# A two-layer diffusion backbone on one NeuronCore: residual stream in two halves, SiLU as one ScalarE function, and constant TensorE products in the stops

## The chip, the cores and the metric

The kernel runs on one core of a Trainium2 chip. The metric is the device time of one execution in microseconds (us); lower is better. Engines are called PE (TensorE), ACT (ScalarE), DVE (VectorE), POOL (GpSimd) and SP (SyncE, which issues most transfers).

## The reference

Two layers over 256 latent and 256 context tokens of width 1024, in float32. Each layer has a mixer (three attention or convolution branches) and a channel mixer, each between two RMS norms, with modulation computed from `c`:

```python
hx = modulate(rmsnorm(x, g_pre_mix[l]), sh1, sc1)
y_x, y_c = mixer_sublayer(hx, hc, ...)
x = x + gt1 * rmsnorm(y_x, g_post_mix[l])
hx = modulate(rmsnorm(x, g_pre_ffn[l]), sh2, sc2)
x = x + gt2 * rmsnorm(channel_mixer(hx, l, ...), g_post_ffn[l])

def swiglu(h, w_gu, w_dn):                  # layer 0, width 2816
    g, u = jnp.split(h @ w_gu, 2, axis=-1)
    return (jax.nn.silu(g) * u) @ w_dn
# layer 1: each token to 2 of 8 experts of width 3584, latent tokens only
```

## The kernel before

Activations lie with channels on partitions: a tensor of width 1024 is 8 tiles (`k`, `KT = 8`) of 128 channels by 512 tokens (latent tokens first, then context). Every product of weights is made in three passes of float32r: ACT copies a weight block to a high part, DVE subtracts it from the raw block to get the low part, and PE multiplies high by high, high by low and low by high. So each 1 MB weight slab goes DMA, ACT (`split_hi` L549, or `hi` L783 for experts), DVE (`split_lo` L835, or `lo` L1230), PE. Five instruction queues are written by hand and joined by semaphores; within a queue the order is that of the code.

The stages, in time: eight slabs of the modulation product `ada` (PE L1307) to 50 us; mixer of layer 0 to 654 us; dense FFN in two halves of 12 and 10 tiles to 1109 us; mixer of layer 1 to 1461 us; router to 1508 us; then a loop over jobs of one expert and 128 token slots (8 jobs in this run, 42 slabs each, 127 us a job) to 2527 us; last norm and output.

Between stages stand norms. `postnorm` (DVE L930 reciprocal, L938, L943) updates the residual `xm` tile by tile; ACT squares each tile (`square`, L584), PE sums it over channels with a product against the constant `mean` (`norm_sum`, L1300, into bank O1; its squares lie in two buffers, so a square waits for the sum two tiles back), ACT takes the root (L578, after a table load), DVE the reciprocal (L896), and `prenorm` scales (DVE L906), shifts (ACT L611) and splits (DVE L917) tile by tile. `first_pair` on PE takes each tile `k` of the split input as soon as it is there, six products a tile. In these stretches PE has nothing to do but wait.

The router (layer 1): 16 transposes of the normed latent tokens (L1546), 16 products with 8 columns for the logits (L1551), a chain of small DVE operations, five products with 8 columns (L1556 to L1560), more small DVE operations, one more product (L1563) and the reading of the job count, then `gather` (16 products, L1571), which builds the tokens of the first job.

SiLU is made as x(1+tanh(x/2))/2: ACT tanh from PSUM (L730 dense, L805 experts), then on DVE two `scalar_tensor_tensor` (L1085 and L1086, or L1253 and L1255). In an expert job the 28 gate/up slabs go in 14 groups `q` of two slabs; in each, DVE does two `lo`, the two SiLU operations, and one split of the transposed result (L1246). The 14 down slabs follow; in the first of them DVE also prepares the one-hot matrices of the next job (L1210 to L1218). Three split buffers (`wse`) stand between ACT/DVE and PE.

The residual `xm` is `[P, KT, TOK]`; its context half is free in the expert stage and serves as the sixth raw slab buffer, eight pieces of 1 KB a partition. The output is written from the latent half, also eight pieces of 1 KB.

Of the kernel before, what the change touches and what calls it, by code (L numbers as in the profile page):

```python
# [28 lines left out]
P = 128  # L29
# [114 lines left out]
def build_program(nc, a, out):  # L144
    ctx = ExitStack()
    with ctx:
# [11 lines left out]
        xm = sb("xm", [P, KT, TOK])  # L158
# [31 lines left out]
        def ada_rows(n):  # L190
# [21 lines left out]
                 view(M, 8192, 8, 256), view(M, 10240, 8, 256), view(M, 12288, 8, 256), xm[:, :, SEQ:TOK]]  # L212
# [50 lines left out]
        tanh_done, gu_taken, hF_done = sem("tanh_done"), sem("gu_taken"), sem("hF_done")  # L263
# [6 lines left out]
        e_tanh, e_h, e_T, e_hThi, e_hT = sem("e_tanh"), sem("e_h"), sem("e_T"), sem("e_hThi"), sem("e_hT")  # L270
# [156 lines left out]
        def _(sp):  # L427
# [74 lines left out]
            sp.dma_start(out, xm[:, :, 0:SEQ]).then_inc(out_done, 16)  # L502
# [37 lines left out]
        def _(act):  # L540
# [39 lines left out]
            def square(src, n, k, N):  # L580

                if 8 * n + k >= 2:
                    act.wait_ge(sum_done, 8 * n + k - 1)
                act.activation(sq[:, k % 2, 0:N], src, ACT.Square).then_inc(sq_done, 1)  # L584

            def ada():
                split_to(1)
                for s in range(ADA_FIRST):
# [3 lines left out]
                    for k in FIRST_NORM[s]:  # L592
                        if k == 0:
                            act.wait_ge(x_in, 16)
                        square(xm[:, k, :], 0, k, TOK)

            def prenorm(n, l, which, N, hcount):
                if n == 0:
                    act.wait_ge(eps_ready, 3)
                else:  # L600
                    for k in range(KT):
                        act.wait_ge(x_upd, 8 * hcount[0] + k + 1)
                        square(xm[:, k, 0:N], n, k, N)
# [115 lines left out]
            def ffn():  # L719
                for h in range(2):  # L720
# [74 lines left out]
            with act.Fori(0, n_jobs) as j:  # L795
# [5 lines left out]
                for q in range(GU_GROUPS):  # L801
# [3 lines left out]
                    act.activation(tge[:, q % 2, :], S[q % 2][:, 0:256], ACT.Tanh, scale=0.5).then_inc(e_tanh, 1)  # L805
# [23 lines left out]
        def _(dve):  # L829
# [64 lines left out]
            def prenorm(n, l, which, N):  # L894
# [3 lines left out]
                for k in range(KT + 1):  # L898
                    if k < KT:
# [4 lines left out]
                        for s in range(ns):  # L904
                            c = slice(SEQ * s, SEQ * s + SEQ)
                            ins = dve.scalar_tensor_tensor(gt[:, k % 2, c], xm[:, k, c], am[:, 2 * which, k, s:s + 1],  # L906
# [20 lines left out]
            def postnorm(n, l, which, N, src):  # L927
# [6 lines left out]
                for k in range(KT + 1):  # L934
# [4 lines left out]
                    if k:  # L939
                        dve.wait_ge(dve_self, at[k - 1])  # L940
                        for s in range(N // SEQ):
                            c = slice(SEQ * s, SEQ * s + SEQ)
                            ins = dve.scalar_tensor_tensor(xm[:, k - 1, c], gt3[:, (k - 1) % 3, c], am[:, 2 * which + 1, k - 1, s:s + 1],  # L943
                                                           xm[:, k - 1, c], ALU.mult, ALU.add)
# [57 lines left out]
            def mixer(l):  # L1002
                nq = TOK if l == 0 else SEQ

                mg = xm if l == 0 else xm[:, :, SEQ:TOK]
# [64 lines left out]
            def ffn():  # L1070
                for h in range(2):
# [6 lines left out]
                    def body(i, last):  # L1078
                        for s in range(2):
# [3 lines left out]
                            dve.wait_ge(tanh_done, f0 + 2 * i + s + 1)  # L1083
# [10 lines left out]
                    body.own_per = 4  # L1094
# [146 lines left out]
            with dve.Fori(0, n_jobs) as j:  # L1241
                own.base, own.jobs_done = start + j * (GU_GROUPS + 10), j + 1
# [22 lines left out]
                assert own.k == GU_GROUPS + 10  # L1265
# [5 lines left out]
            own.base, own.k = start + n_jobs * (GU_GROUPS + 10), 0  # L1271
# [6 lines left out]
        def _(pe):  # L1278
# [528 lines left out]
```

## Time and profile before

| | |
|---|---|
| median of three runs | 2555.19 us (2554.53 to 2555.3) |
| the profiled execution's own time | 2547.89 us |
| its span, first to last instruction | 2545.8 us |
| busy PE / DVE / ACT | 2375.2 / 1746.2 / 1341.0 us |
| mean granted TensorE clock | 0.974 of full |

Busy shares are over the whole span; PE's matmuls are pipelined and their ends are modelled, so a busy PE row can still hide slack of some tenths of a microsecond. The granted clock is 1.00 (2.4 GHz) or 0.50 (1.2 GHz) in any short stretch.

### The profile page before, as it was taken

What the parts mean: (1) busy time and instruction counts of PE and PEld (TensorE: products, weight loads), DVE (VectorE), ACT (ScalarE), POOL (GpSimd) and SP (SyncE); (2) the same over time, 40 slices, a digit from 0 to 9 for tenths busy, and PEclk for the clock granted to TensorE, in tenths of its full rate; (3) what the DMA queues carried; (4) which work ended last, traced back from release to release, by engine and by line L of the source; (5) the groups of instructions that cost most, each with busy time, mean ns of one, the idle gap of its engine ahead of it and who ended that gap; (6) DMA issues with size and microseconds to landing.
All of it is one profiled execution on the core that took longest, in us unless ns stands there. A gap on an engine that the chain in (4) does not pass through costs nothing.

```text
span 2545.8 us, 34852 instructions
## 1 busy us (share of the span) xinstructions
PE 2375.2 (93%) x12536; PEld 1941.4 (76%) x12536; DVE 1746.2 (69%) x2249; ACT 1341.0 (53%) x1636; POOL 28.6 (1%) x26
## 2 busy tenths in 40 slices
PE   5988999999799999978999869999999999999997
PEld 3766877777488788757899858888888888888885
DVE  5565456543655345466656469898989898989897
ACT  5334445432444233234445347676767676767674
POOL 0000000000000000000011000000000000000000
PEclk9989999999899999989999979999999999999999
DMA  6222333333144244313244449898989898989894
GB/s 226 70 97 100 117 108 108 116 116 116 54 161 165 99 144 153 111 55 116 100 130 136 170 152 368 326 369 325 369 326 369 325 369 325 368 326 367 326 367 164
DMA packets 128776, 528.62 MB, mean 208 GB/s; under 512 B 9136, under 2 KB 68016, under 8 KB 75440
## 3 DMA queue, kind: packets, MB, share of 16 engines
q1 hardware_dynamic: 126096, 520.86, 55.9%
q10 hardware_dynamic: 2592, 6.55, 0.8%
q8 instruction: 59, 0.97, 0.1%
q14 instruction: 29, 0.24, 0.0%
HBM read 526.33 MB, written 1.05 MB: 207 GB/s over the span
## 4 chain that ended last, share of the span: by engine, by line
PE 84%; DVE 9%; ACT 4%; issue 2%; DMA 1%; ACTq 0%; DVEq 0%; SPq 0%
PE O L1626 11%; PE pp L1283 9%; PE pp L1284 8%; PE pp L1285 8%; PE S L1604 8%; PE S L1602 8%; PE S L1603 8%; PE pp L1307 3%; PE O L1300 2%; DVE wsp L835 2%; PE S L1283 2%; PE T L1283 1%; PE S L1284 1%; PE T L1284 1%; PE S L1285 1%
## 5 line engine op out<-in xcount | busy, mean ns | idle before, releaser
L835 DVE TENSOR_TENSOR wsp<-raw,wsp 128x1024 fp32r<-128x1024 f32 (+3 forms) x344 | 378.6, 1125 | 477.8 <-ACT wsp L549 473.3
L1230 DVE TENSOR_TENSOR opr<-M,opr 128x2048 fp32r<-128x2048 f32 x168 | 383.5, 2287 | 30.0 <-ACT opr L783 27.1
L549 ACT ACTIVATE wsp<-raw 128x1024 fp32r<-128x1024 f32 (+3 forms) x344 | 322.2, 966 | 122.3 <-PE T L1285 81.2
L783 ACT ACTIVATE opr<-M 128x2048 fp32r<-128x2048 f32 x168 | 322.6, 1920 | 91.9 <-PE O L1626 52.0
L1602 PE MATMUL S<-opr,hx 128*128 128x512 f32 x896 | 359.0, 401 | 2.3 <-DVE hx L1235 2.2
L1604 PE MATMUL S<-opr,hx 128*128 128x512 f32 x896 | 350.3, 391 | 0.0
L1603 PE MATMUL S<-opr,hx 128*128 128x512 f32 x896 | 349.4, 390 | 0.0
L1283 PE MATMUL pp<-hx,wsp 128*128 128x512 f32 (+1 forms) x800 | 286.7, 358 | 41.4 <-DVE wsp L835 15.7
L1626 PE MATMUL O<-opr,wsp 128*128 128x512 f32 x1344 | 311.5, 391 | 12.9 <-DVE opr L1230 12.9
L1626 PEld LDWEIGHTS O<-opr,wsp 128*128 128x128 f32 x1344 | 250.5, 188 | 67.7 <-DVE opr L1230 16.3
L1284 PE MATMUL pp<-hx,wsp 128*128 128x512 f32 (+1 forms) x800 | 279.9, 350 | 0.0
L1285 PE MATMUL pp<-hx,wsp 128*128 128x512 f32 (+1 forms) x800 | 279.4, 349 | 0.0
L1230 DVE TENSOR_TENSOR opr<-raw,opr 128x2048 fp32r<-128x2048 f32 x114 | 261.0, 2290 | 19.5 <-ACT opr L783 14.6
L783 ACT ACTIVATE opr<-raw 128x2048 fp32r<-128x2048 f32 x114 | 219.0, 1921 | 49.2 <-PE O L1626 25.6
L1283 PEld LDWEIGHTS pp<-hx,wsp 128*128 128x128 f32 x800 | 155.5, 194 | 66.9 <-issue 33.3
L1283 PE MATMUL pp<-opr,wsp 128*128 128x512 f32 (+1 forms) x496 | 185.7, 374 | 12.9 <-DVE opr L1065 9.9
L1604 PEld LDWEIGHTS S<-opr,hx 128*128 128x128 f32 x896 | 168.2, 188 | 35.8
L1602 PEld LDWEIGHTS S<-opr,hx 128*128 128x128 f32 x896 | 168.3, 188 | 34.8 <-issue 2.4
L1603 PEld LDWEIGHTS S<-opr,hx 128*128 128x128 f32 x896 | 168.7, 188 | 32.4
L1284 PE MATMUL pp<-opr,wsp 128*128 128x512 f32 (+1 forms) x496 | 177.9, 359 | 0.0
L1285 PE MATMUL pp<-opr,wsp 128*128 128x512 f32 (+1 forms) x496 | 177.7, 358 | 0.0
L1285 PEld LDWEIGHTS pp<-hx,wsp 128*128 128x128 f32 x800 | 155.1, 194 | 19.5
(203 smaller groups left out, 3374.1 us busy)
## 6 DMA issues: line engine op xcount, KB each, us to landing
M<-in_w_moe SPq DMA_DIRECT2D x168, 1024.0 KB, 4.9
raw<-in_w_main SPq DMA_DIRECT2D x132, 1024.0 KB, 4.9
raw<-in_w_moe SPq DMA_DIRECT2D x114, 1024.0 KB, 4.9
xm<-in_w_moe SPq DMA_DIRECT2D x56, 1024.0 KB, 5.7
raw<-in_w_br SPq DMA_DIRECT2D x24, 512.0 KB, 3.6
raw<-in_w_dn SPq DMA_DIRECT2D x8, 768.0 KB, 4.1
raw<-in_w_dn SPq DMA_DIRECT2D x8, 640.0 KB, 3.8
M<-in_rpb_rows ACTq DMA_DIRECT2D x16, 256.0 KB, 2.9
```

Source lines behind the costliest of these rows:

```text
L549: act.activation(wsp[:, slot, 0, 0:w], raw[:, slot // 2, half * w:half * w + w], ACT.Copy).then_inc(hi_done, 1)
L783: act.activation(wse[i % SPLIT_E][:, 0, :, :], raw_e[i % RAW_E], ACT.Copy).then_inc(e_hi, 1)
L835: dve.tensor_tensor(wsp[:, slot, 1, 0:w], raw[:, slot // 2, half * w:half * w + w], wsp[:, slot, 0, 0:w], ALU.subtract).then_inc(lo_done, 1)
L1230: dve.tensor_tensor(w[:, 1, :, :], raw_e[i % RAW_E], w[:, 0, :, :], ALU.subtract).then_inc(e_lo, 1)
L1283: mm(dst, w_hi, x_hi, start=first, stop=False)
L1284: mm(dst, w_hi, x_lo, start=False, stop=False)
L1285: return mm(dst, w_lo, x_hi, start=False, stop=last)
L1307: ins = mm(dst[0:4, 0:256], c4[:, 4 * h + k, :], wsp[:, slots[h], part, 256 * k:256 * k + 256], start=(h + k + part == 0), stop=(h == 1 an ...
L1602: mm(d, xg[0][:, kk, :], wh, start=(kk == 0), stop=False)
L1603: mm(d, xg[0][:, kk, :], wl, start=False, stop=False)
L1604: ins = mm(d, xg[1][:, kk, :], wh, start=False, stop=(kk == KT - 1))
L1626: ins = mm(O[n][:, :].rearrange("p (a b) -> p a b", b=256), hT[x][:, f, :], w[:, part, 4 * f2 + 2 * n:4 * f2 + 2 * n + 2, :], start=(f == ...
```

## The change

1. `xm` becomes `[P, 2, KT, SEQ]`: latent half, then context half, so that each half is 8 KB contiguous in a partition. The host array `x_both` and all readers and writers follow; the sixth expert slab and the output become one row of 8 KB.
2. SiLU: ACT evaluates `Silu` instead of `Tanh`, and DVE has one `tensor_tensor` with the up product instead of two `scalar_tensor_tensor`.
3. `keep_up(n)` puts `n` products of the constant `mean` with itself (128x128, float32) into PSUM bank T1, which nothing reads, at eleven places in PE's queue ahead of a wait.

```diff
-        xm = sb("xm", [P, KT, TOK])
+        xm = sb("xm", [P, 2, KT, SEQ])
...
-                 view(M, 8192, 8, 256), view(M, 10240, 8, 256), view(M, 12288, 8, 256), xm[:, :, SEQ:TOK]]
+                 view(M, 8192, 8, 256), view(M, 10240, 8, 256), view(M, 12288, 8, 256), xm[:, 1, :, :]]
...
-            sp.dma_start(out, xm[:, :, 0:SEQ]).then_inc(out_done, 16)
+            sp.dma_start(out, xm[:, 0, :, :]).then_inc(out_done, 16)
...
-                            act.activation(gt[:, s, :], S[s][:, :], ACT.Tanh, scale=0.5).then_inc(tanh_done, 1)
+                            act.activation(gt[:, s, :], S[s][:, :], ACT.Silu).then_inc(silu_done, 1)
...
-                            own.link(dve.scalar_tensor_tensor(gt[:, s, :], gt[:, s, :], 1.0, S[s][:, :], ALU.add, ALU.mult))
-                            dve.scalar_tensor_tensor(hf2[:, s, :], gt[:, s, :], 0.5, T[s][:, :], ALU.mult, ALU.mult
-                                                     ).then_inc(gu_taken, 1)
+                            dve.tensor_tensor(hf2[:, s, :], gt[:, s, :], T[s][:, :], ALU.mult).then_inc(gu_taken, 1)
...
-                    dve.wait_ge(e_tanh, j * GU_GROUPS + (q + 1))
-                    own.link(dve.scalar_tensor_tensor(tge[:, q % 2, :], tge[:, q % 2, :], 1.0, S[q % 2][:, 0:256],
-                                                      ALU.add, ALU.mult))
-                    dve.scalar_tensor_tensor(hse[:, q % 2, :], tge[:, q % 2, :], 0.5, S[q % 2][:, 256:512],
-                                             ALU.mult, ALU.mult).then_inc(e_h, 1)
+                    dve.wait_ge(e_silu, j * GU_GROUPS + (q + 1))
+                    dve.tensor_tensor(hse[:, q % 2, :], tge[:, q % 2, :], S[q % 2][:, 256:512], ALU.mult).then_inc(e_h, 1)
...
+            def keep_up(n):
+
+                for _ in range(n):
+                    mm(T[1][:, 0:P], mean[:], mean[:], start=True, stop=True)
...
             ada()
+            keep_up(32)
             mixer(0, 1, 0)
+            keep_up(34)
             for k in range(KT):
                 norm_sum(2, k, TOK)
+            keep_up(31)
             ffn()
+            keep_up(32)
             for k in range(KT):
                 norm_sum(4, k, TOK)
+            keep_up(31)
             mixer(1, 5, 2)
+            keep_up(21)
             for k in range(KT):
                 norm_sum(6, k, SEQ)
+            keep_up(31)
...
+            keep_up(11)
             pe.wait_ge(rt_dve, 2)
...
+            keep_up(20)
...
-            gather(0)
+            gather(0, 14)
+            keep_up(8)
```

PE's queue at the router, before (L1300 is `norm_sum`; L1546 the transposes; L1551 the logits; L1556 to L1563 the small products; L1564 reads the job count; L1571 is `gather`):

```order
L1300 MATMUL O<-M,mean 128x256 x10
L1546 MATMUL pp<-ident,M 128x128 x8
L1546 MATMUL S<-ident,M 128x128 x8
L1551 MATMUL O<-wr,M 128x8 x16
L1556 MATMUL O<-M,ctab 128x8
L1557 MATMUL O<-M,ctab 128x8
L1558 MATMUL O<-M,ctab 128x8
L1559 MATMUL O<-M,ctab 128x8
L1560 MATMUL O<-M,ctab 128x8
L1563 MATMUL O<-M,ctab 128x8
L1564 TENSOR_LOAD jobs
```

The same place in the changed kernel, where L1299 is `keep_up`, L1303 `norm_sum`, L1556 the transposes, L1561 the logits, L1567 to L1575 the small products and L1584 `gather`:

```order
L1303 MATMUL O<-M,mean 128x256 x8
L1299 MATMUL T<-mean 128x128 x31
L1556 MATMUL pp<-ident,M 128x128 x8
L1556 MATMUL S<-ident,M 128x128 x8
L1561 MATMUL O<-wr,M 128x8 x16
L1299 MATMUL T<-mean 128x128 x11
L1567 MATMUL O<-M,ctab 128x8
L1568 MATMUL O<-M,ctab 128x8
L1569 MATMUL O<-M,ctab 128x8
L1570 MATMUL O<-M,ctab 128x8
L1571 MATMUL O<-M,ctab 128x8
L1299 MATMUL T<-mean 128x128 x20
```

Nothing is moved there; runs of constant products stand between the old rows, each ahead of a row that waits for DVE or ACT. Behind them, 14 more stand ahead of `gather` and 8 behind it.

ACT's queue at the head of the expert loop, before (L783 is `hi`, L805 the tanh, the other rows registers):

```order
L795 UNCONDITIONAL_BRANCH
L795 ISA
L782 ISA
L783 ACTIVATE opr<-M 128x2048
L782 REGISTER_ALU
L783 ACTIVATE opr<-M 128x2048
L804 REGISTER_ALU
L805 ACTIVATE M<-S 128x256
L783 ACTIVATE opr<-M 128x2048
```

The same place in the changed kernel, where L786 is `hi` and L808 the SiLU:

```order
L798 UNCONDITIONAL_BRANCH
L798 ISA
L785 ISA
L786 ACT_TABLE_LOAD
L786 ACTIVATE opr<-M 128x2048
L785 REGISTER_ALU
L786 ACTIVATE opr<-M 128x2048
L807 REGISTER_ALU
L808 ACT_TABLE_LOAD
L808 ACTIVATE M<-S 128x256
L786 ACTIVATE opr<-M 128x2048
```

Two loads of activation tables have come into the loop's body, ahead of its first `hi` and ahead of its first SiLU; they stand there once a job. In the first dense half's loop (five passes) one load stood ahead of the first `split_hi`; in the changed kernel a second stands ahead of the first SiLU of each pass:

```order
L549 ACT_TABLE_LOAD
L549 ACTIVATE wsp<-raw 128x1024
L548 REGISTER_ALU
L549 ACTIVATE wsp<-raw 128x1024
L732 REGISTER_ALU
L733 ACT_TABLE_LOAD
L733 ACTIVATE M<-S 128x512
```

## Rows read from the trace of the kernel before

**Rows 1.** Stretches: us, busy PE, PEld, DVE, ACT, POOL, clock, DMA share, GB/s.

```profile
658.00:668.00 10.00, 6.11 (x7) 2.38 (x8) 9.96 (x20) 3.04 (x5) 0.00 (x0) 0.50 0.00 0
1477.00:1483.00 6.00, 3.44 (x16) 3.45 (x17) 1.77 (x4) 3.97 (x8) 0.00 (x0) 0.50 0.41 130
1484.00:1487.00 3.00, 3.00 (x28) 2.94 (x27) 0.00 (x0) 1.17 (x1) 0.00 (x0) 1.00 1.00 423
1488.00:1504.00 16.00, 5.73 (x25) 5.57 (x26) 11.15 (x50) 2.12 (x2) 1.80 (x1) 0.50 0.03 14
```

**Rows 2.** Chain that ended last, by time, in the first mixer's `first_pair`.

```profile
64.43 0.88 DVE M L906 x2
...
66.20 0.88 DVE M L906 x2
```

**Rows 3.** Timeline at the FFN start: start, us, engine, line [idle before, releaser].

```profile
670.61 0.63 ACT L584 ACTIVATE M<-xm 128x512 f32<-128x512 f32 x1 [0.41 <-PE O L1300]
690.19 1.28 ACT L549 ACT_TABLE_LOAD   x1
691.49 2.01 ACT L549 ACTIVATE wsp<-raw 128x1024 fp32r<-128x1024 f32 x2
693.88 1.99 ACT L549 ACTIVATE wsp<-raw 128x1024 fp32r<-128x1024 f32 x2
695.00 2.01 PE L1307 MATMUL pp<-wsp,c 128*4 128x256 f32 x16 [1.76 <-DVE wsp L835]
```

**Rows 4.** Timeline of PE, and a row of DVE, last mixer to first expert.

```profile
1466.11 6.39 PE L1300 MATMUL O<-M,mean 128*128 128x256 f32 x16 [4.79 <-ACT M L584]
1469.51 0.88 DVE L943 SCALAR_TENSOR_TENSOR xm<-M,am,xm 128x256 f32<-128x256 f32 x2
1479.56 1.97 PE L1546 MATMUL pp<-ident,M 128*128 128x128 f32 x8 [7.06 <-ACT M L611]
1483.03 4.00 PE L1551 MATMUL O<-wr,M 128*128 128x8 f32 x32
1489.85 0.59 PE L1556 MATMUL O<-M,ctab 128*128 128x8 f32 x2 [2.83 <-DVE M L1164]
1490.30 0.57 PE L1557 MATMUL O<-M,ctab 128*128 128x8 f32 x2
1497.02 0.56 PE L1563 MATMUL O<-M,ctab 128*128 128x8 f32 x2 [4.86 <-DVE M L1202]
1501.13 5.32 PE L1571 MATMUL pp<-M 128*128 128x128 f32 x32 [3.55 <-DVE M L1218]
1508.67 0.49 PE L1602 MATMUL S<-opr,hx 128*128 128x512 f32 x1 [2.22 <-DVE hx L1235]
```

**Rows 5.** Timeline at the end of the first dense half.

```profile
844.00 0.69 DVE L1086 SCALAR_TENSOR_TENSOR M<-M,T 128x512 f32<-128x512 f32 x1
846.23 0.49 PE L1283 MATMUL pp<-opr,wsp 128*128 128x512 f32 x1 [1.20 <-DVE opr L1092]
```

**Rows 6.** Timeline at the head of an expert job.

```profile
1629.29 3.73 PE L1571 MATMUL pp<-M 128*128 128x128 f32 x32
1634.03 1.91 ACT L783 ACTIVATE opr<-M 128x2048 fp32r<-128x2048 f32 x1
1639.24 1.92 ACT L783 ACTIVATE opr<-M 128x2048 fp32r<-128x2048 f32 x1 [3.30 <-PE S L1604]
1641.96 0.38 ACT L805 ACTIVATE M<-S 128x256 f32<-128x256 f32 x1 [0.80 <-PE S L1604]
1644.19 2.29 DVE L1230 TENSOR_TENSOR opr<-M,opr 128x2048 fp32r<-128x2048 f32 x1
```

**Rows 7.** Waits from 1515 to 2525 us: total, times, longest.

```profile
PE O L1626 <- DVE opr L1230: 12.9, 8, 1.6
```

**Rows 8.** DMA issues: KB each, us from issue to landing.

```profile
M<-in_w_moe SPq DMA_DIRECT2D x168, 1024.0 KB, 4.9
...
xm<-in_w_moe SPq DMA_DIRECT2D x56, 1024.0 KB, 5.7
```

More of the change, by code:

```diff
@@ L262, in build_program @@
         bias_in, bias_ready = [sem("bias_in0"), sem("bias_in1")], sem("bias_ready")
-        tanh_done, gu_taken, hF_done = sem("tanh_done"), sem("gu_taken"), sem("hF_done")
+        silu_done, gu_taken, hF_done = sem("silu_done"), sem("gu_taken"), sem("hF_done")
         act_self, dve_self, pool_self = sem("act_self"), sem("dve_self"), sem("pool_self")
@@ L583, in square @@
                     act.wait_ge(sum_done, 8 * n + k - 1)
-                act.activation(sq[:, k % 2, 0:N], src, ACT.Square).then_inc(sq_done, 1)
+                dst = sq[:, k % 2, 0:N]
+                if len(src.shape) == 3:
+                    dst = dst.rearrange("p (a b) -> p a b", b=SEQ)
+                act.activation(dst, src, ACT.Square).then_inc(sq_done, 1)
             def ada():
@@ L594, in ada @@
                             act.wait_ge(x_in, 16)
-                        square(xm[:, k, :], 0, k, TOK)
+                        square(xm[:, :, k, :], 0, k, TOK)
             def prenorm(n, l, which, N, hcount):
@@ L602, in prenorm @@
                         act.wait_ge(x_upd, 8 * hcount[0] + k + 1)
-                        square(xm[:, k, 0:N], n, k, N)
+                        square(xm[:, :, k, :] if N == TOK else xm[:, 0, k, :], n, k, N)
                 norm_root(n, N)
@@ L804, in _ @@
                     act.wait_ge(e_used, j * JOB_SLABS + (2 * q + 2 + SPLIT_E))
-                    act.activation(tge[:, q % 2, :], S[q % 2][:, 0:256], ACT.Tanh, scale=0.5).then_inc(e_tanh, 1)
+                    act.activation(tge[:, q % 2, :], S[q % 2][:, 0:256], ACT.Silu).then_inc(e_silu, 1)
                     if q == 1:
@@ L905, in prenorm @@
                             c = slice(SEQ * s, SEQ * s + SEQ)
-                            ins = dve.scalar_tensor_tensor(gt[:, k % 2, c], xm[:, k, c], am[:, 2 * which, k, s:s + 1],
+                            ins = dve.scalar_tensor_tensor(gt[:, k % 2, c], xm[:, s, k, :], am[:, 2 * which, k, s:s + 1],
                                                            rs[:, c], ALU.mult, ALU.mult)
@@ L942, in postnorm @@
                             c = slice(SEQ * s, SEQ * s + SEQ)
-                            ins = dve.scalar_tensor_tensor(xm[:, k - 1, c], gt3[:, (k - 1) % 3, c], am[:, 2 * which + 1, k - 1, s:s + 1],
-                                                           xm[:, k - 1, c], ALU.mult, ALU.add)
+                            ins = dve.scalar_tensor_tensor(xm[:, s, k - 1, :], gt3[:, (k - 1) % 3, c], am[:, 2 * which + 1, k - 1, s:s + 1],
+                                                           xm[:, s, k - 1, :], ALU.mult, ALU.add)
                             if s == N // SEQ - 1:
@@ L1003, in mixer @@
                 nq = TOK if l == 0 else SEQ
-                mg = xm if l == 0 else xm[:, :, SEQ:TOK]
+                mg = xm[:].rearrange("p s (h k) c -> p (s h) (k c)", k=2) if l == 0 else xm[:, 1, :, :]
                 for row in mixer_steps[l]:
@@ L1093, in body @@
                             dve.wait_ge(hF_done, f0 + 2 * i + s + 1)
-                    body.own_per = 4
+                    body.own_per = 2
                     loop(dve, n, body, own)
@@ L1241, in _ @@
             with dve.Fori(0, n_jobs) as j:
-                own.base, own.jobs_done = start + j * (GU_GROUPS + 10), j + 1
+                own.base, own.jobs_done = start + 10 * j, j + 1
                 def hT_lo(q):
@@ L1264, in _ @@
                 xg_lo(j + 1)
-                assert own.k == GU_GROUPS + 10
+                assert own.k == 10
                 for n in range(4):
@@ L1270, in _ @@
                                       ALU.add).then_inc(e_acc, 1)
-            own.base, own.k = start + n_jobs * (GU_GROUPS + 10), 0
+            own.base, own.k = start + n_jobs * 10, 0
             postnorm(7, 1, 1, SEQ, yacc)
@@ L1564, in _, with gather @@
             n_jobs = pe.value_load(jobs[0:1, 12:13], min_val=1, max_val=MAX_JOBS)
-            def gather(j):
+            def gather(j, idle=0):
+                keep_up(idle)
                 pe.wait_ge(e_onehot, j + 1)
@@ L1782, in _lay_out @@
         "w_main": w_main, "w_br": w_br, "w_dn0": w_dn0, "w_dn1": w_dn1, "w_moe": _pack_experts(inp),
-        "x_both": tok.T.reshape(KT, P, TOK).transpose(1, 0, 2),
+        "x_both": tok.T.reshape(KT, P, 2, SEQ).transpose(1, 2, 0, 3),
         "c_both": np.stack([inp["c"][0], inp["c_ctx"]], axis=1).reshape(KT, P, 2).transpose(1, 0, 2),
```

4 lines of the change are left out of this document (2 added, 2 removed).

## The prediction

> **What bounds the kernel now.** I read the page first: PE is busy for 93% of the span and its mean granted clock is 0.974, so what is left is short waits and a little half-rate work. Then the table of stretches, to find where the clock is low: the long stops between stages and the whole router are at 0.50 [rows 1]. Then the chain that ended last, by time, to see whether the half-rate products are on the path, and the timelines for what follows a stop.
>
> Between stages it is mostly not PE's clock that counts. In the first mixer's `first_pair` the chain goes through DVE, one tile every 1.77 us (64.43 to 66.20) [rows 2]; PE needs for a tile six products of 0.23 us at full clock, 1.4 us, or 2.6 us at half. It starts behind by what the half clock costs and has caught up before the last tile. In the router it is otherwise: PE, DVE and ACT take turns, each waits for the one before, and every half-rate product lies on the path [rows 4]. In the expert stage PE runs nearly without gap; its one wait is 12.9 us in 8 jobs, for a low part that DVE makes late because it builds the one-hot matrices first [rows 7].
>
> **The constant products.** First, do they fit? One is a 128x128 float32 product like those of `gather`: 16 take 3.73 us with the last one's tail at full clock, so 0.223 us each [rows 6]. The eleven runs then take 7.1, 7.6, 6.9, 7.1, 6.9, 4.7, 6.9, 2.5, 4.5, 3.1 and 1.8 us. The stops in the router are 4.79, 7.06, 2.83, 4.86, 3.55 and 2.22 us [rows 4], and of the 3.55 PE spends part on reading the job count; I charge 0.1 us there. The stops between stages of 512 tokens are of the length of the 7.06 one or longer. Nothing else stands in the way: T1 is not read then. Each run starts at full clock, as the clock falls only some microseconds into a stop.
>
> Do they hold the clock? In 658 to 668 us products of the same stationary `mean` ran at 0.50 and the clock came back behind them [rows 1]; `gather`, of the very form of a constant product, started at 0.50 at 1501 and had the clock back at 1504 [rows 1, 4]. I take yes.
>
> What it gives, place by place:
> - The three `first_pair`: nothing where DVE sets the end [rows 2]. The pair of layer 1's mixer, where PE is behind nearly to the last tile, 0.1 us.
> - `norm_sum` at 662 us: the last square waited 0.41 us for PE [rows 3]; I take 0.2. At 1116 us the last square waits for DVE alone: 0. At 1466 us (256 tokens): the last update of `xm` ends at 1470.39, and one square of 0.42 and one sum of 0.45 behind it would end at 1471.3, plus handovers 1471.6, where the sums now end at 1472.5 [rows 4]: 0.9.
> - Transposes and logits: 1479.56 to 1483.03 at half clock [rows 1, 4], 3.47 us for 16 transposes, so 1.7 saved; the half-rate start of the logits adds 0.3. Together 2.0.
> - The five small products go at 0.45 us start to start (1489.85, 1490.30) at half clock; the logits, of the same form, took 4.00 us for 16 at full, 0.24 each [rows 4]. Saved 0.9.
> - `gather`: 5.32 against 3.73 us at full clock [rows 4, 6]: 1.6. ACT and DVE are free behind it, so the first expert product moves with it.
> Sum 5.7, less the 0.1: 5.6 us.
>
> **SiLU.** DVE loses one operation a tile. In the dense loop and in the expert groups PE is the bound, so that is hidden, except at two ends. At the end of a dense half PE waits for the last tile's split, 1.20 us in the first half, with the 0.69 us operation in the chain [rows 5]: 0.7 saved, and 0.65 in the second, whose stop I take as about as long. At the start of the down stage of a job the low part that PE waits for comes after a `hi` of ACT which itself waits for PE, so DVE's new slack is cut to 0.06 us a job: 0.5 in eight.
>
> ACT pays with table loads of 1.28 us [rows 3]: one more in each of five passes of the dense loop, two in each of eight jobs. In a dense pass the second load falls into ACT's wait for the gate tile, 24 products of PE, and is hidden. Not so in the first pass: ACT's highs of 693.88 go to about 695.3 behind load and SiLU, the first low part behind them is ready at 697.6, and PE is done with its modulation product at 697.0 (695.00 + 2.01) [rows 3]. Cost 0.6, once. At a job's head the first load delays the `hi` of 1634.03 to end at 1637.3, when DVE has just become free. The second starts when the `hi` of 1639.24 ends, at 1641.16, and ends at 1642.44 instead of the SiLU's 1641.96: 0.48 us late. The next `hi` (1.92) and `lo` (2.29) then end at 1647.0; PE wants that slab at 1641.96 - 0.2 + 2 x 2.72 + 0.4 = 1647.6 (a slab takes 2.72, the distance of the two ACT waits) [rows 6]. Hidden, with half a microsecond to spare. In the first job, where nothing is prepared ahead, I charge 0.3.
>
> The Trainium skill's "ScalarE: Activation LUTs", section "What ACT_TABLE_LOAD costs", adds a drain of about 1.38 us to each switch, 2.66 us in all, and says to group functions by set. In the row the `split_hi` starts 0.02 us behind the load's end [rows 3], so I let the trace decide; by the rule each job would lose 0.9 us and the sum would shrink by 7.
>
> SiLU itself I take to last as long as tanh (0.38 us) [rows 6]; no row shows it. If it lasted twice that, the head's slack would be just used up: 0 to 1 us.
>
> **Layout.** A slab written in 1 KB pieces lands in 5.7 us, one in 8 KB pieces in 4.9 [rows 8]. In the expert stage nobody waits for it, so 0. The output transfer is last on the path and of the same size: between 0 and 0.8 saved, I take 0.6, near the rows. ACT and DVE read the same number of elements: 0.
>
> **Sum.** 5.6 + 1.35 + 0.5 - 0.6 - 0.3 + 0.6 = 7.15 us. The profiled execution took 2547.89 us, 2545.8 of it span; 2540.7 after. The runs shown have a median 7.3 us above that execution, so 2548.0 us.
>
> **Rivals.**
> - *The clock falls inside the router.* [...] If it lasts one run: 11 x 0.446 - 2.83 = 2.1 over, and 0.9 not gained: 2551. If it stays low to `gather`: 2.1 + (8.9 - 4.86) + (6.2 - 3.55) + (3.6 - 2.22) = 10.2 over and 2.5 not gained, which ends at 2548.0 + 12.7 = 2560.7, slower. It decides against the change once the clock stays low through the second run. [...] Against: 31 constant products stand ahead and the clock came back at `gather`.
> - *The constant products don't hold the clock at all*, the change does not do what it says. Then all eleven overrun, 4 to 8 us in each of seven long stops: above 2590. Against: rows 1.
> - *The table loads reach the path.* Half a microsecond of slack at each head; with a load of 2.66 instead of 1.28, 0.9 x 8 = 7 us lost: 2555, no change.
> - *PE was held by its clock more than the chain shows*, so that each of the five half-rate stretches gives another microsecond: 2543.
>
> The Trainium skill's "TensorE: Matmul & The Clock Gate", section "Part 4: PE-mode transpose", says that a transpose does not count as busy to the clock gate; with the transposes and logits in a row that would speak for the first rival, and give its 2551. In the trace the clock rose behind the transposes at 1483 [rows 1], which speaks against it.
>
> **Numbers.** Forecast 0.53; one fall in the router 0.13; low to `gather` 0.08; no hold 0.04; loads on the path 0.12; more gain 0.10. The range goes from 2543.5 to 2555. About 0.2% (5.1 us) can be told from no change here: faster below 2550.1. The forecast falls there in nine cases of ten, the extra gain always, the single fall in one of three: 0.63. Slower: low to `gather` and no hold: 0.12. Same: 0.25.
>
> **What would show it.** After: clock 1.00 from 1461 us to the end of the router and the router some 5.5 us shorter; `first_pair` as long as before; 33 table loads; jobs still 127 us apart; an idle PE of under 1 us at each dense half's end. Wrong if the clock is 0.50 in any run of constant products, if jobs come at 128 us, or if the spacing of tiles in `first_pair` changes.

## The result, and the profile after

| | before | after |
|---|---|---|
| median, first comparison (4 runs each) | 2555.24 us (2554.53 to 2555.3) | 2540.46 us (2539.94 to 2541.04) |
| profiled execution | 2547.89 us | 2541.04 us |
| its span | 2545.8 us | 2538.6 us |
| mean granted clock | 0.974 | 0.989 |
| busy PE / DVE / ACT | 2375.2 / 1746.2 / 1341.0 us | 2424.3 / 1693.7 / 1368.0 us |

The ratio is 0.9943, 95% interval 0.9926 to 0.996: 14.8 us less, where 7.2 were forecast, and 2540.46 lies below the range of 2543.5 to 2555. Yet the two profiled executions differ by 6.85 us, close to the forecast sum of 7.15. The step from the one to the other is taken up below; a part of the 14.8 us stays unexplained.

The table of stretches of after, at the places of [rows 1] and the stretch ahead of the router (columns as there):

```profile
658.00:668.00 10.00, 8.66 (x34) 4.00 (x32) 10.00 (x23) 3.78 (x6) 0.00 (x0) 1.00 0.00 0
1461.00:1477.00 16.00, 15.71 (x110) 12.82 (x110) 12.55 (x26) 7.37 (x17) 0.00 (x0) 1.00 0.07 17
1477.00:1483.00 6.00, 5.87 (x54) 5.68 (x53) 0.42 (x2) 4.25 (x7) 0.00 (x0) 1.00 0.63 240
1484.00:1487.00 3.00, 2.73 (x26) 2.54 (x24) 2.38 (x15) 0.20 (x1) 0.00 (x0) 1.00 1.01 418
1488.00:1504.00 16.00, 14.78 (x121) 14.09 (x121) 10.78 (x39) 5.47 (x5) 1.81 (x1) 1.00 0.18 67
```

The clock is 1.00 where it was 0.50. The timeline of PE through the router, to be laid beside [rows 4] (L1299 is `keep_up`):

```profile
1470.80 7.08 PE L1299 MATMUL T<-mean 128*128 128x128 f32 x62
1478.02 1.09 PE L1556 MATMUL pp<-ident,M 128*128 128x128 f32 x8
...
1479.82 3.64 PE L1561 MATMUL O<-wr,M 128*128 128x8 f32 x32
1483.31 2.70 PE L1299 MATMUL T<-mean 128*128 128x128 f32 x22
1486.28 0.39 PE L1567 MATMUL O<-M,ctab 128*128 128x8 f32 x2 [0.27 <-DVE M L1165]
```

Eight transposes take 1.09 us, not 1.97. The runs fit their stops: 0.27 us is left ahead of the small products. From the first transpose to the first small product it is 8.3 us (10.3 before), from there to the first expert product 16.3 (18.8 before). From the first square (1464.87) to the first expert product (1502.57) the router now takes 37.7 us, and 43.0 before.

In the first mixer's `first_pair` DVE's tiles come as they did in [rows 2], 1.78 us apart (timeline of DVE):

```profile
64.19 0.88 DVE L909 SCALAR_TENSOR_TENSOR M<-xm,am,M 128x256 f32<-128x256 f32 x2
65.96 0.88 DVE L909 SCALAR_TENSOR_TENSOR M<-xm,am,M 128x256 f32<-128x256 f32 x2
```

The dense stage's start, timeline of ACT and one row of PE, beside [rows 3]:

```profile
688.47 1.28 ACT L549 ACT_TABLE_LOAD   x1
689.76 2.01 ACT L549 ACTIVATE wsp<-raw 128x1024 fp32r<-128x1024 f32 x2
691.78 1.28 ACT L733 ACT_TABLE_LOAD   x1
693.08 0.60 ACT L733 ACTIVATE M<-S 128x512 f32<-128x512 f32 x1
...
693.27 2.01 PE L1310 MATMUL pp<-wsp,c 128*4 128x256 f32 x16 [1.90 <-DVE wsp L838]
```

Two loads stand where one stood, and each is followed 0.01 or 0.02 us behind its end by the next ACTIVATE. The trace of after has 35 loads (14 before; 33 were forecast). The first product of the down stage of the first half waits 0.46 us where it waited 1.20 [rows 5]:

```profile
844.68 0.49 PE L1281 MATMUL pp<-opr,wsp 128*128 128x512 f32 x1 [0.46 <-DVE opr L1093]
```

The head of an expert job (timeline of ACT), beside [rows 6], then the waits of PE in the expert stage beside [rows 7], then the transfers beside [rows 8], and the output transfer:

```profile
1628.40 1.28 ACT L786 ACT_TABLE_LOAD   x1
...
1633.48 1.92 ACT L786 ACTIVATE opr<-M 128x2048 fp32r<-128x2048 f32 x1 [1.88 <-PE S L1618]
1635.42 1.28 ACT L808 ACT_TABLE_LOAD   x1
1636.71 0.38 ACT L808 ACTIVATE M<-S 128x256 f32<-128x256 f32 x1
```

```profile
PE O L1640 <- DVE opr L1231: 12.6, 8, 1.6
```

```profile
M<-in_w_moe SPq DMA_DIRECT2D x168, 1024.0 KB, 4.9
...
xm<-in_w_moe SPq DMA_DIRECT2D x56, 1024.0 KB, 5.0
...
out_x<-xm SPq DMA_DIRECT2D x1, 1024.0 KB, 3.9
```

SiLU lasts as long as the tanh, 0.38 us. The slab in `xm` lands in 5.0 us (5.7 before), the output in 3.9. The first operation of DVE's preparation of a next job, in the first and in the eighth job, before and then after (timeline of DVE):

```profile
1594.07 0.28 DVE L1210 TENSOR_SCALAR M<-ctab,M 128x128 f32<-128x128 f32 x1
...
2483.17 0.28 DVE L1210 TENSOR_SCALAR M<-ctab,M 128x128 f32<-128x128 f32 x1
```

```profile
1588.32 0.28 DVE L1211 TENSOR_SCALAR M<-ctab,M 128x128 f32<-128x128 f32 x1
...
2477.02 0.28 DVE L1211 TENSOR_SCALAR M<-ctab,M 128x128 f32<-128x128 f32 x1
```

Seven jobs take 889.10 us before and 888.70 after: 0.06 us less each, as forecast.

Two stretches changed in a way that was not forecast. The first mixer (from its first weights to the first square behind it) takes 603.9 us before and 600.8 after, the second (from the first square ahead of it to the first behind it) 350.0 and 351.6. The traces of e1, e4 and e9 below have the same signs: 603.6 and 349.7 in e1, the kernel before, 601.8 and 354.4 in e4, 602.1 and 354.4 in e9, the changed kernel. No run here isolates the cause.

### The profile page after: what moved, and what is told of

Its sections match the earlier page's. It is cut to its first block, busy times and chain, and to the rows that moved or that the text cites. A ratio compares the mean times of both kernels' runs of the same rounds, so it can differ in the third digit from the quotient of the medians.

```text
span 2538.6 us, 35669 instructions
## 1 busy us (share of the span) xinstructions
PE 2424.3 (95%) x13066; PEld 1987.4 (78%) x13066; DVE 1693.7 (67%) x2115; ACT 1368.0 (54%) x1657; POOL 27.0 (1%) x26
## 4 chain that ended last, share of the span: by engine, by line
PE 81%; DVE 11%; ACT 4%; issue 3%; DMA 0%; ACTq 0%; DVEq 0%; SPq 0%
PE O L1640 11%; PE pp L1281 8%; PE S L1618 8%; PE S L1616 8%; PE S L1617 8%; PE pp L1283 8%; PE pp L1282 8%; PE pp L1310 3%; DVE wsp L838 2%; PE S L1281 2%; PE S L1283 2%; PE T L1283 2%; PE T L1281 1%; PE S L1282 1%; PE T L1282 1%
## 5 line engine op out<-in xcount | busy, mean ns | idle before, releaser
L786 ACT ACTIVATE opr<-M 128x2048 fp32r<-128x2048 f32 x168 | 322.5, 1920 | 81.0 <-PE O L1640 51.5
L1283 PE MATMUL pp<-hx,wsp 128*128 128x512 f32 (+1 forms) x800 | 277.0, 346 | 0.0
L786 ACT ACTIVATE opr<-raw 128x2048 fp32r<-128x2048 f32 x114 | 219.1, 1922 | 48.2 <-PE O L1640 25.6
L1281 PE MATMUL pp<-opr,wsp 128*128 128x512 f32 (+1 forms) x496 | 186.0, 375 | 10.7 <-DVE opr L1068 9.3
L1283 PE MATMUL pp<-opr,wsp 128*128 128x512 f32 (+1 forms) x496 | 178.1, 359 | 0.0
L1283 PEld LDWEIGHTS pp<-hx,wsp 128*128 128x128 f32 x800 | 153.6, 192 | 18.9
```

The costliest lines, as they stand in the source:

```text
L786: act.activation(wse[i % SPLIT_E][:, 0, :, :], raw_e[i % RAW_E], ACT.Copy).then_inc(e_hi, 1)
L1281: mm(dst, w_hi, x_hi, start=first, stop=False)
L1283: return mm(dst, w_lo, x_hi, start=False, stop=last)
```

## The experiments

Each session timed its kernels on one chip beside the kernel before, which thus has four more sets of runs: medians 2552.86 (26 runs), 2554.24 (22), 2555.98 (11) and 2554.16 (11).

### First session: the parts alone

e1 is the kernel before with no edit. e2 has only part 3 of the change (the `keep_up` calls), e3 only parts 1 and 2 (layout and SiLU), e4 all of it:

```diff
 # e3, and so at all eleven places
-            keep_up(32)
             mixer(0, 1, 0)
-            keep_up(34)
...
 # e2, the same calls put into the kernel before
+            keep_up(32)
             mixer(0, 1, 0)
+            keep_up(34)
```

> The kernel before, unchanged. The forecast's sum (7.15 us) fits the two profiled executions (2547.89 to 2541.04), yet the timed runs of before lie at 2555. Theory A: before has executions of two kinds that differ only in where the clock falls; then some of these runs lie near 2548 and some near 2555, with spans 7 us apart and a lower mean clock in the longer ones. Theory B (rival): the profiled execution of before was a stray; all runs here lie at 2555 and the profile too. Then the forecast's step from span to median was right, and the change is worth 14 us by something the sum doesn't hold.

> Constant products alone, at all eleven places; tanh and the old layout stay. My sum: 5.6 us off a like execution of before. If theory A holds (clock falls vary from run to run), the gain over the median is 5.6 + 7 = 12 to 13 us, since these products take away most of the falls: about 2542 to 2543, and all runs agree within 1 us. If the additional gain is not the clock's, 2549.5.

> Layout and SiLU as in the changed kernel, no constant products. My sum: 1.55 us off before. Theory A: 2553.7 in the runs of the longer kind (2546 in a short one), with as many clock falls as before. Rival: if SiLU or the layout is what the sum lacks, 2546 in all runs.

> All three parts, the changed kernel again on the same chip as the others: 2540.5, runs within 1 us.

| | median (runs) | ratio to before | profiled: span, clock |
|---|---|---|---|
| e1, before | 2554.72 (11) | 1.0006 [0.9997, 1.0015] | 2550.3, 0.972 |
| e2, constant products | 2544.89 (9) | 0.9968 [0.9958, 0.9978] | 2542.3, 0.989 |
| e3, layout and SiLU | 2553.78 (11) | 1.0 [0.9991, 1.0009] | 2553.5, 0.970 |
| e4, all | 2543.63 (6) | 0.9969 [0.9957, 0.9981] | 2540.3, 0.989 |

e1 came out as neither theory says: its executions and the 26 beside them make no two groups 7 us apart but lie spread over 11 us, at granted clocks of 0.970 to 0.974. e2 missed: 8.0 us less and not 12 to 13, and its nine runs lie 7.4 us apart and not 1. e3's median is as expected. e4 missed: 3.1 us above the expected time, its runs 4.4 us apart and not 1.

The constant products hold nearly the whole gain. Here it is 9.2 us by medians, not 14.8, and the 26 executions of before lie between 2548.04 and 2558.88 us: the profiled execution of before, 2547.89, was shorter than all of them (three of the later sessions were shorter still). e1's profile shows one place where executions of this kernel differ. Stretches of e1 in the router, beside the lower three of [rows 1] (same columns):

```profile
1477.00:1483.00 6.00, 2.13 (x10) 2.14 (x11) 2.67 (x7) 4.08 (x10) 0.00 (x0) 0.64 0.12 31
1484.00:1487.00 3.00, 3.00 (x17) 3.00 (x15) 0.00 (x0) 2.21 (x3) 0.00 (x0) 0.50 1.03 434
1488.00:1504.00 16.00, 6.04 (x27) 5.79 (x27) 8.51 (x48) 2.12 (x2) 1.80 (x1) 0.50 0.13 53
```

And the timeline of PE there:

```profile
1482.63 1.91 PE L1546 MATMUL S<-ident,M 128*128 128x128 f32 x8
1484.34 6.83 PE L1551 MATMUL O<-wr,M 128*128 128x8 f32 x32
```

In [rows 1] the clock was back at 1.00 in 1484 to 1487 us and the logits took 4.00 us; in e1 it stays at 0.50 and they take 6.83. e1's router takes 46.3 us, 3.3 more than in the profiled execution of before, and the first mixer's first weights are loaded at 59.34 instead of 57.32 us. That is 5.3 us, of which the span shows 4.5; the rest comes back in the mixers. e3's router is like e1's, 46.9 us with the clock at 0.50 through it. e6's, which has no constant products in the router either, is like that of the profiled before: 43.1.

### Second session: where the constant products work, and the table loads

e5 has the old layout and SiLU with the five router runs only, e6 with the six runs between stages only; e7 is the whole change with an early SiLU of one element; e8 is the new layout and SiLU with the four runs behind the logits only.

```diff
 # e5: only these; e6: only the other six; e8: only the last four of these
+            keep_up(31)                     # ahead of the transposes
+            keep_up(11)                     # behind the logits
+            keep_up(20)
+            gather(0, 14)
+            keep_up(8)
```

```diff
 # e7
+        dum = sb("dum", [P, 2])
...
                 norm_root(n, N)
+                if n == 2:
+                    act.activation(dum[:, 0:1], eps[:], ACT.Silu)
...
             act.activation(rt[:, 8:10], rt[:, 10:12], ACT.Exp).then_inc(rt_act, 1)
+            act.activation(dum[:, 1:2], eps[:], ACT.Silu)
```

> The old layout and the old SiLU, constant products only behind the last norm sum and in the router (31, 11, 20, 14, 8). Theory (the gain lies in the router, and is larger than forecast since a usual execution has the clock low there from 1479 to 1509 us, while the profiled one had it back at 1484): 6.5 to 8.5 us less than the kernel before in the same session, router stretches of 13.1, 8.3 and 16.3 us from the last square to the first expert product, as with all eleven runs. Rival (half of the gain comes from the stops between stages): 3 to 5 us less. Rival (as forecast): 5.4 us less.

> The old layout and the old SiLU, constant products only at the six places between stages (32, 34, 31, 32, 31, 21), none in the router behind the norm sums. Theory (DVE sets the end of these stretches, only the norm sums gain): 0.5 to 1.5 us less than the kernel before in the same session; the router as without the change, its clock low for some 30 us. Rival (PE was held by its clock more than the chain shows, about a microsecond in each of five stretches): 4 to 6 us less.

> The whole change, and a SiLU of one element a partition behind the root of the FFN's norm and behind the router's Exp, so that the SiLU table is loaded where ACT waits for DVE, and no load is left in the dense loop or the job loop (33 loads become 12). Theory (a load costs only where it stands on the chain: at the dense stage's start, 0.9 for the second one and up to 1.3 for the first, and 0.5 in the first job): 1.4 to 2.7 us less than the whole change alone, so 10.6 to 12 us less than the kernel before where the whole change alone gives 9.2; jobs as far apart as before. Rival (loads in the job loop cost 0.3 us or more a job): jobs closer by 0.3 us or more and 4 us less than the whole change. Rival (the loads are all hidden): no difference to the whole change.

> The new layout and SiLU, constant products only from behind the logits on (11, 20, 14, 8), none ahead of the transposes or between the stages. Theory A (the transposes and logits run at half clock, and the following products are dense enough that the clock comes back within the first two runs): the 11 products take up to 4.9 us in a stop of 2.8, small products start up to 2.1 us late, and from the third run on nothing is late: 0 to 3 us more than with the 31 products ahead. Theory B (8-column and short products never bring it back once low): all four runs overrun and the first expert product comes 10 us later than in the whole change.

- **e5**: 2546.73 us, 7.5 less than before; ratio 0.9972 [0.9963, 0.9981]. The router alone gives most of the gain, more than the 5.3 by which the two profiled executions differ there. Its small products came 10.7 us behind the transposes and not the expected 8.3, since the clock fell within the logits and the eleven constant products behind them ran at half rate (5.04 us).
- **e6**: 2551.64 us, ratio 0.9995 [0.9985, 1.0005]. The runs between stages give no difference that can be told, which fits the 0.5 to 1.5 us expected; the rival's 4 to 6 us lie outside the interval. They do hold the clock, and DVE's tiles come 1.78 us apart still (stretches, then the timeline of DVE, of e6):

```profile
60.00:70.00 10.00, 9.41 (x37) 6.21 (x36) 9.21 (x21) 5.21 (x12) 0.00 (x0) 1.00 0.00 1
655.00:665.00 10.00, 9.58 (x71) 7.79 (x69) 8.83 (x13) 2.92 (x5) 0.00 (x0) 1.00 0.00 0
```

```profile
62.29 0.88 DVE L906 SCALAR_TENSOR_TENSOR M<-xm,am,M 128x256 f32<-128x256 f32 x2
64.07 0.88 DVE L906 SCALAR_TENSOR_TENSOR M<-xm,am,M 128x256 f32<-128x256 f32 x2
```

- **e7**: 2542.38 us, 11.9 less than before; ratio 0.9958 [0.9945, 0.9971]. The table is loaded while ACT waits, and the dense loop starts without a load (timeline of ACT, then of PE):

```profile
671.62 1.28 ACT L610 ACT_TABLE_LOAD   x1
...
688.54 1.99 ACT L550 ACTIVATE wsp<-raw 128x1024 fp32r<-128x1024 f32 x2
690.92 0.60 ACT L736 ACTIVATE M<-S 128x512 f32<-128x512 f32 x1 [0.39 <-PE S L1287]
```

```profile
692.03 2.02 PE L1313 MATMUL pp<-wsp,c 128*4 128x256 f32 x16 [0.47 <-DVE wsp L842]
```

  PE's wait ahead of the modulation product falls from 1.90 to 0.47 us. From the first square to the first product of the down stage it is 2.05 us less than in after, the first job is 0.5 shorter, and jobs are as far apart as in after (seven in 888.72 us): behind the first job, the loads in the job loop cost nothing. The trace has 11 loads.
- **e8**: one run, 2544.92 us, span 2543.0. Transposes at half clock (1.97 and 1.91 us), small products 11.5 us behind the start of the transposes, the first expert product 27.7 us behind it, 3.1 more than in after. Its second run of constant products fits its stop again (4.71 us). Theory A, at its upper end. The clock rose within the logits, at about 1483.5 us, as in the profiled before, fell within the eleven constant products (4.33 us) and was back at their end; what was lost ahead of them stays lost.

### Third session: the whole change again, and the stops it leaves out

e9 is the changed kernel, e10 is e7's kernel, e12 has the new layout and SiLU and only the 31 products ahead of the transposes. e11 is e7's kernel with three runs more:

```diff
                 for s in range(ADA_FIRST):
+                    keep_up(14 if s == 2 else 0)
...
                             if i == 0:
+                                keep_up((20, 15)[l])
                                 pe.wait_ge(m_split, 8 * (l + 1))
```

> The whole change once more, beside the kernel before on the same chip. Theory (the first comparison, 14.8 us, met executions of before at the long end of their spread and of after at the short end; the change itself is worth about 9): 8 to 11 us less than the kernel before, median 2542 to 2545. Rival (the change is worth 14.8 and the second session was the odd one): 13 to 16 us less.

> The whole change with the SiLU table loaded ahead of both loops, once more, on the same chip as the whole change alone. Theory (the loads cost 2.0 at the dense stage's start and 0.5 in the first job): 2 to 3 us less than the whole change alone. Rival (what the two profiles differ in is chance): within 1 us.

> The kernel with the loads ahead of the loops, and constant products at three stops more: 14 ahead of the third slab of the modulation product (a stop of 3.9 us near 17 us), 20 and 15 ahead of each mixer's last stage (5.0 and 4.3 us, near 600 and 1430 us). Theory (every fall of the clock in a stop is followed by half-rate work that PE does not make up): no fall at 17, 597 and 1430 us, the end of the first stage at 56.6 instead of up to 58.9 us, 2 to 4 us less than without them, and a smaller spread. Rival (DVE and ACT set the pace there too): the falls vanish and the time stays.

> The new layout and SiLU, and of the constant products only the 31 ahead of the transposes. Theory A (they keep the clock through the transposes and, mostly, the logits, and it falls in the stop behind): transposes at 1.04 us for eight, not 1.97; the small products and the gather at half, so that the first expert product comes 2.5 to 3.5 us later than in the whole change. Theory B (the transposes and logits bring it down at once, as a rule on transposes says): logits at half, 2 us more.

- **e9**: 2544.50 us (6 runs), 11.5 less than before; ratio 0.9956 [0.9944, 0.9968]. Median as expected, the difference half a microsecond above. Its router takes 38.8 us against 37.7 in after: the clock fell within the eleven constant products, at about 1486.9 us, and was back at about 1490.3, within the small ones. These start 0.8 us later behind the transposes than in after, without a wait, and lose another 0.3 (timeline of PE):

```profile
1482.19 3.64 PE L1560 MATMUL O<-wr,M 128*128 128x8 f32 x32
1485.68 3.97 PE L1298 MATMUL T<-mean 128*128 128x128 f32 x22
1489.44 0.43 PE L1566 MATMUL O<-M,ctab 128*128 128x8 f32 x2
```

  In e7, e10, e13 and e15 the clock fell for as long, and the router takes 38.8 us too; in after, e2, e4 and e14 it did not fall.
- **e10**: 2541.77 us, 2.7 less than e9 beside it; ratio to before 0.9952 [0.9938, 0.9965]. As expected. The intervals of the two overlap, so that it is the stretches that speak for it: 2.05 and 0.5 us, alike in e7 and e10.
- **e11**: 2533.52 us (5 runs), 22.5 less than before; ratio 0.9913 [0.99, 0.9926]. Expected were 2 to 4 us less than e10, measured 8.3: the sign was right, the size wrong. Its profiled execution, 2538.84 us, was the longest of its five. The clock fell at about 1478.7 us, in the middle of the logits, although PE had run nearly without a gap through constant products, transposes and logits (stretches, then the timeline of PE):

```profile
1472.00:1478.60 6.60, 6.46 (x59) 6.27 (x58) 1.33 (x4) 5.17 (x9) 0.00 (x0) 1.00 0.53 189
1478.80:1485.40 6.60, 6.60 (x33) 6.60 (x33) 2.82 (x17) 1.69 (x3) 0.00 (x0) 0.50 0.66 277
```

```profile
1475.90 4.29 PE L1566 MATMUL O<-wr,M 128*128 128x8 f32 x32
1480.04 5.04 PE L1302 MATMUL T<-mean 128*128 128x128 f32 x22
```

  The small products start 2.5 us later behind the transposes than in after, and the router takes 40.4 us, 2.7 more.
- **e12**: one run, 2546.64 us. Transposes and most of the logits ran at full clock (stretches), then, at about 1484.4 us and still within the logits, it fell: the first expert product came 28.5 us behind the transposes' start, 4.0 more than in after, where 2.5 to 3.5 were expected.

```profile
1480.00:1483.00 3.00, 2.87 (x27) 2.87 (x27) 0.00 (x0) 2.24 (x6) 0.00 (x0) 1.00 0.57 183
1484.00:1487.00 3.00, 2.54 (x15) 2.44 (x14) 0.36 (x3) 0.19 (x1) 0.00 (x0) 0.56 1.03 429
1488.00:1504.00 16.00, 6.22 (x27) 6.06 (x28) 10.73 (x47) 2.11 (x2) 1.81 (x1) 0.50 0.08 32
```

### Fourth session: what the executions differ in

e13 is e7's kernel with the 14 constant products alone, e15 with the two runs of the mixers alone, e14 is e11's kernel again.

```diff
 # e13                                      # e15 has the other line alone
+                    keep_up(14 if s == 2 else 0)
```

> The kernel with the loads ahead of the loops and of the three new stops only the one near 17 us (14 constant products). Theory (a fall costs about 0.35 us per microsecond at half clock): the kernel with the loads ahead of the loops has one or more falls there in most executions, so 1 to 2.5 us less than its 2542, and its first mixer starts at 55.4 us. Rival (the stop is bound by transfers): no difference.

> All three new stops once more, for the profile of another execution. Theory (falls in the other stops of the mixers, 3.4 us at a time, come by chance): median 2532 to 2537; an execution 5 us shorter than the 2538.84 one has some 15 us less at half clock, and the two mixers and the router hold the whole difference. Rival (transfers): the difference lies elsewhere, with the same stretches at half clock.

> The kernel with the loads ahead of the loops and constant products ahead of each mixer's last stage (20 and 15), none near 17 us. Theory (falls of 3.4 to 6.8 us there at 0.35 each): 2 to 5 us less than its 2542. Rival (ACT and DVE set the pace of that stage): no difference.

- **e13**: 2540.64 us (6), ratio 0.995 [0.9936, 0.9964]; **e15**: 2538.29 us (6), ratio 0.994 [0.9926, 0.9953]; **e14**: 2534.00 us (6), ratio 0.9926 [0.9912, 0.9939]. The 2542 of the expectations was measured on other chips. Against the kernel before of their own session the three are 13.5, 15.9 and 20.2 us less, where e7's kernel was 11.9 and 14.2 less: for the stop near 17 us alone (e13) no gain is shown, and the gain of the mixers' stops alone (e15) is 2 to 4 us and within the intervals. Within the session, all three stops (e14) are 6.6 us below e13 and 4.3 below e15. How the gain divides isn't settled: in the profiles of e11 and e15 the second mixer is shorter than in e7 and e10 (350.8 and 349.0 us against 351.6 and 353.0), the first is not (602.9 and 603.4 against 601.1 and 602.1).
- The profile of e14 is of an execution of 2532.49 us, 6.35 shorter than e11's of the same kernel. The preparation of the second job starts in e11 and then in e14 at (timeline of DVE):

```profile
1586.60 0.28 DVE L1215 TENSOR_SCALAR M<-ctab,M 128x128 f32<-128x128 f32 x1
```

```profile
1580.25 0.28 DVE L1215 TENSOR_SCALAR M<-ctab,M 128x128 f32<-128x128 f32 x1
```

  So the whole difference lies ahead of the expert stage. The stretches of the first mixer and of the router, in e11 and then in e14, differ in the clock; the FFN and the second mixer between them have 1.00 and 0.99 in both.

```profile
50.00:655.00 605.00, 571.79 (x3214) 453.43 (x3213) 314.06 (x612) 242.72 (x454) 12.05 (x8) 0.98 0.29 104
...
1455.00:1494.00 39.00, 37.71 (x267) 33.94 (x267) 21.42 (x74) 16.81 (x30) 1.80 (x1) 0.91 0.25 94
```

```profile
50.00:655.00 605.00, 571.53 (x3247) 454.38 (x3247) 317.73 (x617) 242.77 (x455) 12.04 (x8) 0.99 0.29 104
...
1455.00:1494.00 39.00, 37.48 (x296) 33.91 (x296) 24.77 (x81) 15.52 (x29) 1.80 (x1) 1.00 0.25 93
```

  The first mixer ends (first square of the residual) at 658.3 us in e11 and 655.0 in e14, and from the transposes to the first expert product it is 27.3 and 24.6: 3.3 and 2.7, together 6.0 of the 6.35. In the whole execution e14 has 18 us less at half clock than e11. The rival with the transfers falls.

## Why the prediction was wrong, step by step

**The step that failed is the last of the sum: "The runs shown have a median 7.3 us above that execution, so 2548.0 us."** It carried the distance between before's profiled execution and its other runs over to after, as if every kernel had it. What the runs show in its place: after's median is 0.6 us below its profiled execution, e4's 1.5 and e9's 0.5 above theirs. The 7.3 belonged to one draw of before: that kernel takes 2546.75 to 2559.78 us in 69 executions beside the experiments (one of 6074.73 us is left out), and 2547.89 is near the short end. A part of the distance can be half-rate work that the change takes away: in e1, 3.3 us of it stood in the router. How the whole 7.3 divides no run shows. Without this step the sum gives 2540.7; after's profiled execution took 2541.04. That agreement is between two single executions and partly luck: after began 1.5 us later (first weights of the first mixer at 58.85 instead of 57.32), its first mixer was 3.1 us shorter and its second 1.5 longer, none of which was forecast (e4 and e9 have the same signs in the mixers).

**How large the gain is.** Three comparisons (the first, e4 and e9) gave 14.8, 9.2 and 11.5 us, with overlapping intervals. The terms give 7.2, and 3.3 more where the clock doesn't come back in before's router: 10.5 us, or 9.4 where the clock falls once, for 3.4 us, in after's (an estimate from the routers of e1 and e9). The 14.8 came from four runs of after near the short end of its own spread (2539.94 to 2541.04, against 2542.12 to 2546.56 in e4 and e9). Why those four lay together isn't settled, and with it what of the 14.8 is the change's.

**The constant products**, 5.6 forecast. In the router, right against the profiled execution: 43.0 to 37.7, 5.3 forecast (0.9 + 2.0 + 0.9 + 1.6, less the 0.1). By part: 0.8 ahead of the transposes (0.9), 2.0 from them to the small products (2.0), 2.5 from there to the first expert product (0.9 + 1.6). Against an execution such as e1's it is 8.6, since the price of the transposes and logits was read from rows in which the clock had come back; of the four profiled executions without constant products in the router, two (e1, e3) are of this kind and two (before, e6) of the other. e5 and e6 confirm the places: 7.5 us from the router, none that can be told from between the stages, where DVE sets the end.

**SiLU.** The first dense half's end gave 1.20 - 0.46 = 0.74 (0.7 forecast), a job 0.06 as forecast, 0.4 in seven. The second half's end gave the 0.65 forecast with some luck: its stop was 0.66 us (L1283 at 1046.53), not "about as long" as the first, and it is gone. The first dense half as a whole became 0.18 us longer (166.72 to 166.90 from its first product to the first of the down stage) in spite of the 0.74, so the first pass lost 0.9, where 0.6 were forecast: PE waits 1.90 and not 1.76 us ahead of its modulation product, and 0.66 us behind it, where it did not wait. Both loads stand on the chain there. e7 took 2.05 us back by moving them, these 0.9 and 1.1 that the kernel before pays too. The first job lost 0.4 us against before and is 0.5 shorter in e7 (0.3 forecast). The Trainium skill's rule of "ScalarE: Activation LUTs", section "What ACT_TABLE_LOAD costs", that a drain comes on top of each load, isn't borne out: the next ACTIVATE starts within 0.02 us of the load's end, and jobs are as far apart with two loads as with none (e7).

**Layout.** From the start of the last update of `xm` (2539.67 before, 2533.47 after) to the end of the span it was 6.1 us and is 5.2: 0.9 saved, 0.6 forecast, above the upper bound of 0.8. Issue (0.64 to 0.35 us) and landing (4.8 to 3.9) both shrank. In the expert stage nothing, as forecast. By time alone e3 can't be told from before.

**The rivals.** A single fall inside the router was given 0.13; it is what most executions have. Of eleven profiled executions with constant products at all places of the router, five (e7, e9, e10, e13, e15) had the clock low for 3.4 us, at a cost of 1.1, two (e5, e11) for 6.8 us, at a cost of 2.7, close to the rival's 3.0, and four (after, e2, e4, e14) not at all. The rival took 0.446 us for a constant product at half clock; in e11 they come 0.43 apart. A clock low to `gather`, and no hold at all, did not occur in any of the eleven. The loads did not reach the jobs' path. "PE held by its clock more than the chain shows" gave nearly the right time, 2543, for a wrong reason: in `first_pair` DVE's spacing did not change. On transposes (the Trainium skill, "TensorE: Matmul & The Clock Gate", section "Part 4: PE-mode transpose") the runs don't decide: from half clock it came back behind them, within the logits, in the profiled before and not in e1; from full clock it fell within the logits in e11 and e12, and not at all in after, and no run has the transposes without the logits.

**The range.** It rested on unknown costs and rivals, all read from one execution. The spread of the executions of before, 13 us, wasn't in it: the three runs shown lay 0.8 us apart, and the profiled one 7 away from them, which was the sign.

## What to carry to other kernels

Before adding a difference to a median, ask what the profiled execution owes its distance from the median to, and whether the change removes just that: a profile is one draw, and where the clock falls in stops it can be an unusual one. Constant products pay in stops whose following work PE itself paces (the router here; three more such stops, at the start and in the mixers, by the medians of e11 and e14), and gave nothing that can be told where DVE paces the end; their count must fit the stop at the lower clock too, where the clock may fall. A table load costs only where its engine is on the chain, so use the new function once on a dummy in an earlier wait. The version that came of it (e11, e14) took 2533.52 and 2534.00 us; the first is 11.0 us less than the whole change beside it (e9).

## What the runs showed of the hardware that was not expected

- The executions of one kernel on one core spread with their granted clock. e10: 2539.88 us at 0.989 and 2547.64 at 0.985; e11: 2532.20 at 0.993 and 2538.84 at 0.990. A clock lower by 0.001 is 5.1 us more at half rate in 2540, so each microsecond at half rate cost about 0.4 us in these two (7.8 / 20.3 and 6.6 / 15.2), an estimate from clocks that are rounded to 0.001. Two profiles give it more directly: the dense stage of e6, with the clock at 0.50 for 6.8 us behind its two modulation products' waits (from 695.7 and 849.3 us), takes 457.4 us, and that of e2, with none, 454.2: 0.47 a microsecond.
- The same work with the same stops may lose the clock in one execution and keep it in another: behind the logits it fell in e9 and not in e4, kernels with the same instructions.
- The profiled executions of e7's kernel and of its variants differ in the start, the mixers and the router alone: e7, e10, e11, e13, e14 and e15 take 451.8 or 451.9 us for the dense stage (first square to first square) and 1035.6 us from the first expert product to the end, each.
- The transposes and logits of e1, 10 us of PE without a gap at half rate, ended with the clock still at 0.50, while in the profiled before it rose within them.
- The clock can fall while PE works: within the logits in e11 (1.00 to 1478.6 us, 0.50 from 1478.8), e5 and e12, and within the constant products in e8 and e9, which took 4.33 and 3.97 us for eleven, between the 2.70 of after and the 5.04 of e11.
